# The first block's attention: products with the values alternate between the two maps of a step

## The reference, cut to what matters

```python
# stick: per head, queries against keys, a mask, then
w = jnp.where(mask, jnp.exp(jax.nn.log_sigmoid(z) + between), 0.0)
return jnp.einsum('bhqk,bkhd->bqhd', w, vf)            # 4 heads of 64
# soft: per head, the chosen keys only
p = jax.nn.softmax(s, axis=-1)
return jnp.einsum('bhqk,bqkhd->bhqd', p, v_sel)        # 4 heads of 64
# diff: one result per head from two maps of scores
p = attn_map(q1b, k1f) - lam * attn_map(q2b, k2f)
return jnp.einsum('bhqk,bkhd->bqhd', p, vf)            # 4 heads of 128
```

## Time and profile before

| | |
|---|---|
| median of 3 runs (lowest to highest) | 2823.17 us (2822.75 to 2827.2) |
| profiled execution | 2823.4 us |
| its span, first to last instruction | 2821.6 us |
| PE busy | 2661.5 us (94%), 14358 passes |
| PEld busy | 2142.8 us (76%) |
| DVE busy | 1541.9 us (55%) |
| ACT busy | 1035.8 us (37%) |
| POOL busy | 331.7 us (12%) |
| mean granted TensorE clock | 0.966 |
| data moved | 239.01 MB, mean 85 GB/s |

### The profile page before, as it was taken

One profiled execution on the slowest core, in us unless ns is written; L12 is line 12 of the kernel. 1 busy time (PEld: TensorE's weight loads), 2 busy tenths in 40 slices (PEclk: granted clock), 3 DMA queues, 4 the chain that ended last, 5 costly groups with the idle time before them and its releaser, 6 DMA issues.

```text
span 2821.6 us, 35708 instructions
## 1 busy us (share of the span) xinstructions
PE 2661.5 (94%) x14358; PEld 2142.8 (76%) x14358; DVE 1541.9 (55%) x2537; ACT 1035.8 (37%) x1807; POOL 331.7 (12%) x270
## 2 busy tenths in 40 slices
PE   7999999999999999998889999989998899899998
PEld 6788888899998867866567777856766578688886
DVE  3787654455445446477647886445743554433444
ACT  3365444433223242234443223343232333322322
POOL 0043310012222010010012221020000000100001
PEclk8999999999999999999889999999999999999999
DMA  3211111122232331320025663322221122223322
GB/s 123 68 46 53 53 61 58 64 83 90 91 96 90 97 120 46 122 65 2 1 87 175 201 194 123 96 95 68 68 67 45 38 82 90 81 91 97 96 92 74
DMA packets 70850, 239.01 MB, mean 85 GB/s; under 512 B 12212, under 2 KB 13109, under 8 KB 70430
## 3 DMA queue, kind: packets, MB, share of 16 engines
q1 hardware_dynamic: 63054, 208.88, 23.3%
q10 hardware_dynamic: 7632, 27.86, 2.9%
HBM read 234.06 MB, written 2.64 MB: 84 GB/s over the span
## 4 chain that ended last, share of the span: by engine, by line
PE 61%; DVE 12%; ACT 3%; issue 2%; POOL 1%; ACTq 0%; DVEq 0%; POOLq 0%
PE ps L574 51%; DVE wl L365 2%; PE ps L2704 2%; ACT wh L359 1%; PE ps L3367 1%; DVE xl L655 1%; PE ps L1770 1%; PE ps L1754 1%; PE ps L1781 1%; DVE arena L3060 1%; DVE arena L1033 1%; PE ps L1619 1%; POOL arena L735 0%; DVE arena L3426 0%; DVE xl L653 0%
## 5 line engine op out<-in xcount | busy, mean ns | idle before, releaser
L574 PE MATMUL ps<-xh,wh 128*128 128x512 f32 (+1 forms) x2728 | 1022.3, 389 | 35.4 <-DVE xl L680 14.8
L574 PE MATMUL ps<-xl,wh 128*128 128x512 f32 (+1 forms) x2728 | 995.0, 379 | 0.0
L574 PE MATMUL ps<-xh,wl 128*128 128x512 f32 (+1 forms) x2728 | 991.2, 378 | 0.0
L365 DVE TENSOR_TENSOR wl<-ring,wh 128x1024 fp32r<-128x1024 f32 x374 | 471.1, 1260 | 650.2 <-ACT wh L359 649.5
L359 ACT ACTIVATE wh<-ring 128x1024 fp32r<-128x1024 f32 x374 | 395.3, 1057 | 992.9 <-PE ps L574 885.3
L574 PEld LDWEIGHTS ps<-xh,wh 128*128 128x128 f32 x2728 | 504.2, 190 | 172.9 <-issue 53.4
L574 PEld LDWEIGHTS ps<-xl,wh 128*128 128x128 f32 x2728 | 502.8, 190 | 100.7 <-issue 9.6
L574 PEld LDWEIGHTS ps<-xh,wl 128*128 128x128 f32 x2728 | 503.9, 191 | 98.3
L2000 PE MATMUL ps<-xh,wh 128*128 128x264 f32 (+1 forms) x816 | 260.4, 319 | 9.6 <-DVE xl L424 9.6
L735 POOL TENSOR_TENSOR arena<-arena 128x512 f32<-128x512 f32 (+1 forms) x42 | 71.5, 1707 | 1422.3 <-ACT arena L719 1422.3
L2000 PE MATMUL ps<-xl,wh 128*128 128x264 f32 (+1 forms) x816 | 235.2, 288 | 0.0
(11 more groups left out here) (386 smaller groups left out, 2790.7 us busy)
## 6 DMA issues: line engine op xcount, KB each, us to landing
ring<-in_weights SPq DMA_DIRECT2D x374, 512.0 KB, 3.5
arena<-in_w_ada ACTq DMA_DIRECT2D x48, 512.0 KB, 4.6
arena<-in_cmp_w SPq DMA_DIRECT2D x2, 2048.0 KB
h<-in_x ACTq DMA_DIRECT2D x4, 528.0 KB, 6.3
arena<-strip_scratch SPq DMA_DIRECT2D x8, 264.0 KB, 3.7
out_features<-arena SPq DMA_DIRECT2D x8, 256.0 KB, 2.1
con<-in_consts SPq DMA_DIRECT2D x1, 777.0 KB, 11.1
arena<-in_c ACTq DMA_DIRECT2D x1, 512.0 KB, 3.6
```

The lines of the kernel that those rows point to most:

```text
L365: dve.tensor_tensor(flat(self.wl[:, s % 2]), flat(self.ring[:, s % RING]), flat(self.wh[:, s % 2]).bitcast(F32), ALU.subtract).then_inc(se ...
L574: last = pe.matmul(self.place(u, e), w[:, k, :], x[:, k, o:o + m], start=(k == 0 and i == 0), stop=(k == self.chunks - 1 and i == 2))
```

## The change

The loop over blocks of keys moves outside the loop over maps. The products with the meta tokens' values come first for both maps, then the products of each block for both maps. The number of products, their operands, the order of summation in each map and the increment on the last product stay as they were. Behind L2540 the changed kernel's lines are one further down.

```diff
             pe.wait_ge(self.kept.sem, self.kept.at(self.t_before[s + 1]))
             self.values_ready(pe, s)
             out, blocks = ps[:, 4, 0:nq], nk // P
-            for m in range(x.maps):
-                part = slice(64 * m, 64 * m + 64) if x.maps == 2 else slice(0, P)
+            parts = [slice(64 * m, 64 * m + 64) for m in range(2)] if x.maps == 2 else [slice(0, P)]
+            for m, part in enumerate(parts):
                 last = pe.matmul(out[part], x.VM[0:32, x.v, part], self.PM[0:32, m * nq:(m + 1) * nq], start=True, stop=(blocks == 0))
-                for j in range(blocks):
+            for j in range(blocks):
+                for m, part in enumerate(parts):
                     last = pe.matmul(out[part], x.VT[:, j, x.v, part], self.PT[:, m, j * nq:(j + 1) * nq], start=False,
                                      stop=(j == blocks - 1))
             last.then_inc(self.out_ready.sem, 1)
```

## The result

The changed kernel takes 2805.82 us (median of 4 runs, 2805.34 to 2807.1), the kernel before 2822.96 us beside it (4 runs, 2822.61 to 2827.2). The ratio is 0.9934 (95% interval 0.9905 to 0.9963), the difference 17.1 us. The forecast was 2808.1 us, a saving of 15.3. Of the rivals' times none lies near. By the ratio, the kernel of the first table would take 0.9934 x 2823.17 = 2804.5 us, the lower end of the range: more was gained than the sum held. The interval of the ratio is 16 us wide, so the times alone don't tell a gain of 15.3 us from one of 17.1. The profiles have to.

A forecast was written before the change was run, and what follows sets the result against it. TensorE, busy 94% of the span, was taken to bound the kernel. Its list shortens by 16.64 + 0.52 = 17.2 us, less 1.85 in waits: 15.3 us off 2823.4 gives 2808.1 us, range 2804.5 to 2814.

The forecast's parts named there:

- TensorE's list, 17.2 us: First block's 16 two-map steps with blocks: shorter passes save 16.64 us, plus 0.52 for one step at half clock.
- The 0.14 us for a change of shape: Inside a step: switching between 32-row and 128-row products was taken to cost TensorE about 0.14 us.
- Both maps overlap: First block's attention: adjacent products of two maps, in different column halves, take one map's time; further block 0.217 us, not 0.437.
- The relay's share, 1.85 us: Stick steps: TensorE waits for GpSimd's squares in the square, sum, root, refine chain, losing 1.15 + 0.70 us.
- The two-block step at 170: Stick step at 170 us: saves 0.93 us and keeps it, since GpSimd's square leaves 1.08 us slack at 175.26.
- the stick steps: First block, 140 to 275 us: of 8.8 us saved there, 7.0 us were to arrive.
- The soft steps, all 8.3 us: First block, 437 to 545 us: GpSimd has little work and sets no cap, so all 8.3 us arrive.
- The total: Whole kernel: 15.3 us off the profiled execution's 2823.4 us gives 2808.1 us.
- rivals 3 and 4: Half-clock stretches: one more costs at most 4.4 us, 2812.5 us (chance 0.08); four cost 17.6, 2825.7 us (chance 0.02).
- a crumb of 0.02 on the gaining side: Whole kernel: chance 0.02 of gaining above 17.2 us, as when a half-clock stretch disappears.
- Rival 1: Two-map steps: no overlap, only fewer changes of shape, 4.5 us saved, 2818.9 us; chance 0.03.
- Rival 2: Stick and soft steps: more of the gain turns into waits, 10.2 us saved, 2813.2 us; chance 0.15.

The follow-up runs named there:

- the third experiment: Changed kernel, with the meta tokens' products taking all 128 rows (32 to 127 zero) instead of 32: 2803.57 us, ratio 0.9921.
- the seventh experiment: Changed kernel plus idle ScalarE copies at the first block's end: 4 copies 2810.51 us, ratio 0.9954; 10 copies 2806.32 us, ratio 0.9946.

## Why the prediction was right or wrong

**TensorE's list, 17.2 us: right.** The steps were forecast at 0.73, 0.95, 1.16 and 1.38 us and 1.23 at half clock. They measured 0.734, 0.952, 1.170, 1.388 and 1.246. What carried this was a row of the same shape in the next block and a slope taken from steps of different length. The 0.14 us for a change of shape was inferred from one distance, and the third experiment measured it directly.

**Both maps overlap: right, and the sentence of the Trainium skill against it doesn't hold here.** "TensorE: Matmul & The Clock Gate", section "Part 3: Packing small matmuls — row/col tiling", would let a weight load overlap only when it goes to other rows. Four passes of 128 rows that differ in columns take 0.37 us, as two of one map did. The same section's table has three products packed by columns run 2.38 times as fast, which fits this trace, so the rival rested on one sentence of it. The same section says that matmuls start in the order of the program. For the fp32 products of these traces that doesn't hold: with four blocks map by map, map 1's first pass starts at 200.85 us, ahead of the last three of map 0's eight (200.95 to 201.17), which stand before it in the program.

**The relay's share, 1.85 us: right for GpSimd, too small for the waits as a whole.** TensorE's waits for GpSimd at 187 and 209 us (now 184.15 and 205.79) grew by 0.98 and 0.97 us, 1.95 together, and the total at L2362 came to the 5.6 us forecast. In starts of instructions the two places cost 1.05 and 1.14 us, where 1.15 and 0.70 were forecast. "The two-block step at 170 saves 0.93 and keeps it" failed: at 177.13 us (now 174.23) the second half of the same item waits 0.71 us for ScalarE's copy (L2373) in place of 0.18, and 0.54 us are lost. The forecast had looked at GpSimd's slack alone. What covered this up is luck. The stretch at half clock at 153.6 us lasted 6.8 us in place of 10.2 in both profiles of the changed kernel, which gave 1.1 us in the first, and 0.6 of these were lost again at the next wait for ScalarE. So 8.9 us of shorter steps, 3.3 of waits and 1.1 of clock make the 6.6 us of the stick steps, forecast as 7.0.

**The soft steps, all 8.3 us: right.** 8.2 in the changed kernel and 8.24 with the soft steps alone.

**The first block: 15.2 and 14.8 us in two profiles, forecast 15.3.** The sum is met, but in part because the 1.5 us more of waits met 1.1 us from the clock (the diff steps, where nothing was changed, add 0.3 in one profile and -0.1 in the other).

**The total: the step that failed is the one that wasn't written.** "Against the profiled execution ... that gives 2808.1 us" takes it that all stages behind the first block move as they stand. They don't. In the changed kernel the stages from the merging stage to the second block's attention took 689.0 us in place of 695.7, that attention 190.4 in place of 185.9, at a clock of 0.84 in place of 0.87, with the same instructions. Busy times of the kernel before and of the changed one, in that order:

```profile
544.00:1239.70 695.70, 676.64 (x4057) 579.12 (x4057) 373.80 (x512) 233.20 (x327) 98.73 (x73) 0.98 0.29 93
1239.70:1425.60 185.90, 161.50 (x1354) 109.00 (x1355) 127.88 (x445) 90.93 (x263) 11.28 (x33) 0.87 0.02 7
```

```profile
528.20:1217.20 689.00, 670.40 (x4057) 574.78 (x4057) 373.62 (x511) 233.00 (x327) 98.73 (x73) 0.99 0.30 94
1217.20:1407.60 190.40, 166.25 (x1356) 112.05 (x1355) 127.84 (x445) 91.14 (x263) 11.21 (x33) 0.84 0.02 7
```

That is -6.7 and +4.5 us, and with the rest 2.0 more saved. The change in the first block moved their start, and the seventh experiment shows that a delay without any change of work can do as much: there the attention starts at 1222.5 us and not at 1218.3, and its 190.3 us are 185.8 again. TensorE's time at the lower level in the two rows above went from 26 to 13.5 us and from 50 to 60. So about 2 us of the 17.1 stand in both profiles of this program and have nothing to do with what the edit saves. The forecast had this as a risk on the losing side (rivals 3 and 4) and as a crumb of 0.02 on the gaining side. The effect has both signs, and it should have stood as several microseconds to either side of the sum, with the lower end of the range nearer to 2802.

**The rivals.** Rival 1 (no overlap) fell by the 0.73 us step. Rival 2 (more waits) fell as it was priced, at 10.2 us. It was right in kind: beside the squares, waits for ScalarE took 0.5 to 1.1 us. Experiment 3 shows that it is near, since there 9 us of list bring 2 to 4 us. Rivals 3 and 4: the lower clock stood for less time than before, 185 us in place of 195, and not for more.

## What to carry to other kernels

Where two products write different halves of the output partitions from different columns of the array, put them next to one another in the order: their passes run side by side for one another's price, as long as no more than about four passes of one lie between. Whether it is worth anything is read from the stage: here it was 15 us where TensorE hands out the time. In the second block its undoing lengthened TensorE's list by 7 us and the end time didn't show it. Give each item of a relay the slack towards every engine that it waits for, and not only the slowest. Compare kernels whose stages begin at other times by the stage that was changed, and keep several microseconds to either side for the stages behind it.

## What the runs showed of the hardware

- fp32 passes of two products that differ only in their columns overlap wholly: four take 0.37 us, two of one product 0.35.
- The overlap reaches about four passes back in the program: two blocks map by map lose nothing (0.95 us), three lose 0.27 and four 0.49 us.
- A change between products of 32 and of 128 rows costs 0.14 to 0.15 us. Filling up to 128 rows is free beside it: 0.59 in place of 0.73 us, and 0.36 in place of 0.65 for a step of the diff kind.
- The stretches at the lower clock level, 175 to 199 us in a span of 2.8 ms, fall at nearly the same places in two profiles of one program (starts within 0.4 us for the kernel before, about 1 us for the changed one, with one stretch elsewhere in each pair) and at others when a stage is moved by a few microseconds. One stage of 186 us changes by 4.5 us through that. In eleven profiles a microsecond at the lower level made two unchanged stages 0.4 to 0.45 us longer.
